# The first blocks of the triangular system made straight from PSUM, and the VectorE order of one head around them

## What is computed

```python
decay = jnp.exp(jnp.where(incl, gc[..., :, None] - gc[..., None, :], -jnp.inf))
k_beta = k * beta[..., None]
lower = jnp.where(strict, jnp.einsum('bnhid,bnhjd->bnhij', k_beta, k) * decay, 0.0)
sol = lax.linalg.triangular_solve(eye + lower, rhs, left_side=True, lower=True, unit_diagonal=True)
...
w_dec = sol[..., dv:]
k_dec = k * jnp.exp(gc[..., -1:] - gc)[..., None]
```

## Time and profile before

| | |
|---|---|
| median of 3 runs | 2103.08 us (2101.87 to 2104.11) |
| the profiled execution's own time | 2103.87 us |
| its span in the profile | 2102.2 us |
| TensorE matmul busy | 2072.2 us, 99% |
| TensorE weight load busy | 1687.8 us, 80% |
| VectorE busy | 1245.4 us, 59% |
| ScalarE busy | 804.9 us, 38% |
| GpSimd busy | 745.1 us, 35% |
| granted TensorE clock | 0.998 of full |
| share of the chain that ended last | PE 95%, VectorE 2%, DMA 1%, ScalarE 1% |

### The profile page before, as it was taken

The page is one execution under the profiler, slowest core; times in us unless marked ns, Lnnn a source line. Parts: engine busy times, 40 slices in busy tenths (PEclk is TensorE's granted clock), DMA queues, the critical chain, the costliest instruction groups (busy, mean ns, idle before and its releaser), DMA issues.

```text
span 2102.2 us, 30578 instructions
## 1 busy us (share of the span) xinstructions
PE 2072.2 (99%) x12076; PEld 1687.8 (80%) x12076; DVE 1245.4 (59%) x1739; ACT 804.9 (38%) x1055; POOL 745.1 (35%) x555
## 2 busy tenths in 40 slices
PE   6999999999999999999999999999999999999998
PEld 6789888887787787877878778777778888888886
DVE  6543243348779597795978959776433435454333
ACT  5433232344444443434434344453242222222223
POOL 0000000028577485774857748567201000100000
PEclk9999999999999999999999999999999999999999
DMA  8244343443433434334343343443356565553334
GB/s 257 62 125 131 105 130 90 115 118 97 118 101 96 119 96 116 101 99 120 95 114 102 104 115 100 110 116 101 105 165 205 171 188 151 175 152 110 114 123 148
DMA packets 382913, 260.63 MB, mean 124 GB/s; under 512 B 23769, under 2 KB 351810, under 8 KB 382146
## 3 DMA queue, kind: packets, MB, share of 16 engines
q1 hardware_dynamic: 364146, 203.16, 35.6%
q0 software_dynamic: 11408, 43.00, 6.0%
q10 hardware_dynamic: 7232, 12.72, 1.6%
HBM read 223.17 MB, written 27.28 MB: 119 GB/s over the span
## 4 chain that ended last, share of the span: by engine, by line
PE 95%; DVE 2%; DMA 1%; ACT 1%; issue 1%; POOLq 0%; ACTq 0%; DVEq 0%
PE bank L450 29%; PE bank L452 28%; PE bank L451 28%; PE bank L1089 1%; PE bank L848 1%; PE bank L863 1%; DMA yst<-s_out 1%; PE bank L971 1%; PE bank L983 1%; DVE wl L444 1%; PE bank L1038 0%; PE bank L1079 0%; PE bank L944 0%; PE bank L1052 0%; PE bank L1027 0%
## 5 line engine op out<-in xcount | busy, mean ns | idle before, releaser
L450 PE MATMUL bank<-uh,wh 128*128 128x512 f32 x2048 | 828.2, 404 | 3.3 <-DVE wl L444 2.9
L452 PE MATMUL bank<-uh,wl 128*128 128x512 f32 x2048 | 799.4, 390 | 0.0
L451 PE MATMUL bank<-ul,wh 128*128 128x512 f32 x2048 | 799.0, 390 | 0.0
L444 DVE TENSOR_TENSOR wl<-raw,wh 128x1024 fp32r<-128x1024 f32 x352 | 468.7, 1334 | 495.8 <-ACT wh L436 494.2
L436 ACT ACTIVATE wh<-raw 128x1024 fp32r<-128x1024 f32 x352 | 370.6, 1058 | 558.1 <-DMA raw<-in_w_in_dram 185.9
L450 PEld LDWEIGHTS bank<-uh,wh 128*128 128x128 f32 x2048 | 384.7, 188 | 92.3 <-issue 11.4
L452 PEld LDWEIGHTS bank<-uh,wl 128*128 128x128 f32 x2048 | 384.4, 188 | 83.3
L451 PEld LDWEIGHTS bank<-ul,wh 128*128 128x128 f32 x2048 | 385.2, 188 | 74.9 <-issue 2.9
L616 POOL DMA_DIRECT2D gated_c<-ox x8 | 4.3, 543 | 378.3 <-DVE ox L1780 377.8
L657 POOL TENSOR_TENSOR hr<-tcos,gr 128x512 f32<-128x512 f32 x32 | 51.7, 1617 | 199.4 <-DVE gi L2107 199.2
L1441 ACT ACTIVATE gk<-bank 128x512 f32<-128x512 f32 x48 | 28.7, 598 | 191.6 <-PE bank L452 191.5
(11 more groups left out here) (341 smaller groups left out, 2774.7 us busy)
## 6 DMA issues: line engine op xcount, KB each, us to landing
raw<-in_w_in_dram SPq DMA_DIRECT2D x224, 512.0 KB, 3.9
raw<-in_w_kv_mem_dram SPq DMA_DIRECT2D x32, 512.0 KB, 4.0
raw<-in_w_out_dram SPq DMA_DIRECT2D x32, 512.0 KB, 3.6
gates<-gk ACTq DMA_DIRECT2D x48, 256.0 KB, 4.3
gates<-gates POOLq DMA_DIRECT2D x24, 512.0 KB, 4.7
raw<-in_s_w_glu_dram SPq DMA_DIRECT2D x16, 512.0 KB, 4.0
raw<-in_w_br_c_dram SPq DMA_DIRECT2D x16, 512.0 KB, 4.0
raw<-in_w_br_a_dram SPq DMA_DIRECT2D x16, 512.0 KB, 3.9
```

What stands on the lines that cost most here:

```text
L444: dve.tensor_tensor(k.wl[slot][:, c], k.raw[slot][:, c], k.wh[slot][:, c].bitcast(F32), ALU.subtract).then_inc(k.w_lo, 1)
L450: pe.matmul(o, ah, bh, start=start, stop=False)
L451: pe.matmul(o, ah, bl, start=False, stop=False)
L452: return pe.matmul(o, al, bh, start=False, stop=stop)
```

## The change

It does three things.

1. `system` no longer makes all of `dl`. It makes the four 32-row diagonal strips of `lb` straight from bank 7 and `dl` (four multiplies of 32 x 128), and `first_blocks` loses its four copies. The full product into `dl` is a new function `masked_keys`. The order on VectorE becomes `system`, `first_blocks`, `masked_keys`, `keys`, `values`.
2. The copies `s5h`, `hph`, `dh` and `cwh` are gone; the instructions read the columns of `s5p`, `hp`, `prm2` and `prm1` at the head's index.
3. GpSimd's `arguments(0)` waits for the constant `s5_formed`, counted once before the mixer, in place of `sliced`. The count of `s5_w` is 12 for each head in place of 13.

```diff
 def system(j):
     dve.wait_ge(k.kk, count(j, 1, 1))
     dve.wait_ge(k.pm, count(j, 2, 4))
+    wait(dve, k.lx, count(j, 0, 6))
+    for r in range(0, P, B):
+        tt(k.lb[r:r + B, :, :], chunked(ps[7][:, :])[r:r + B, :, r:r + B], k.dl[r:r + B, :, r:r + B],
+           ALU.mult).then_inc(k.tu_s, 1)
+
+def masked_keys(j):
+    dve.wait_ge(k.tu_s, count(j, 4, 8))
     tt(k.dl[:, :, :], chunked(ps[7][:, :]), k.dl[:, :, :], ALU.mult).then_inc(k.lm, 1)

 def first_blocks(j):
-    dve.wait_ge(k.lm, count(j, 1, 1))
-    wait(dve, k.lx, count(j, 0, 6))
-    for r in range(0, P, B):
-        dve.tensor_copy(k.lb[r:r + B, :, :], k.dl[r:r + B, :, r:r + B]).then_inc(k.tu_s, 1)
     dve.wait_ge(k.tu_s, count(j, 4, 8))
     dve.transpose(k.lbt[:, :, :], k.lb[:, :, :]).then_inc(k.tu_s, 1)
...
-        if j: keys(j); system(j); values(j); first_blocks(j)
+        if j: system(j); first_blocks(j); masked_keys(j); keys(j); values(j)
...
-        if j: head_parameters(j)
...
-    wait(dve, k.ysum, count(j, 0, 1))
-    dve.tensor_copy(k.dh[:, :], k.prm2[:, 96:104][:, bass.ds(at(j), 1)]).then_inc(w, 1)
...
-        if heads: conv_weights(a); convolve(a, 0)
+        if heads: convolve(a, 0)
...
 # GpSimd, arguments(q)
-            hi_, lo_ = k.s5h[:, 1, q:q + 1], k.s5h[:, 2, q:q + 1]
+            hi_, lo_ = (k.s5p[:, n, 4 * at(j) + q:4 * at(j) + q + 1] for n in (1, 2))
...
-                wait_apart(k, pool, k.sliced, count(j, 2, 2))
+                pool.wait_ge(k.s5_formed, 2)
```

More of the change, by code:

```diff
@@ L205, in build @@
             k.zbs = sb(area, "zbs", [S])
-            k.cwh = sb(area, "cwh", [CONV, 3])
             k.braw = sb(area, "braw", [2, 4, GS])
@@ L230, in build @@
             k.st = sb(area, "st", [P])
-            k.hph = sb(area, "hph", [4, NT])
             k.hk = sb(area, "hk", [4, NT])
-            k.s5h = sb(area, "s5h", [5, 4])
-            k.dh = sb(area, "dh", [1])
             k.xb = sb(area, "xb", [S])
@@ L309, in build @@
             sems("mx_out", "zb_st", "pad_zero", "z_kept")
[L311 to L314, removed]
+        k.tu_zero, = \
+            sems("tu_zero")
+        k.s5_formed, k.conv, k.silu, k.sq, k.osum, k.grow_s = \
+            sems("s5_formed", "conv", "silu", "sq", "osum", "grow_s")
         k.grow_st, k.rsum, k.root, k.er_s, k.dd, k.dec, k.rn = \
@@ L537, in s5_loads @@
     def s5_loads(j):
-        wait_apart(k, sp, k.s5_w, count(j, 0, 13))
+        wait_apart(k, sp, k.s5_w, count(j, 0, 12))
         for n, b in enumerate((k.b_re, k.b_im)):
@@ L1061, in s5_matrices @@
     def s5_matrices(j):
-        pe.wait_ge(k.s5_w, count(j, 13, 13))
+        pe.wait_ge(k.s5_w, count(j, 12, 12))
         pe.wait_ge(k.bp_l, count(j, 2, 2))
@@ L1463, in input_halves @@
     def input_halves(j):
-        act.wait_ge(k.s5_w, count(j, 9, 13))
+        act.wait_ge(k.s5_w, count(j, 8, 12))
         wait(act, k.s5_tr, count(j, 0, 1))
@@ L1816, in s5_factors @@
             step(tt(T(11), T(11), T(12), op))
-            step(tt(k.s5p[:, 3 + n, :], T(11), T(9), ALU.mult))
+            tt(k.s5p[:, 3 + n, :], T(11), T(9), ALU.mult).then_inc(k.s5_formed, 1)
+            dve.wait_ge(k.s5_formed, n + 1)
     def delta_parameters():
@@ L1891, in rep_chunks @@
         return m.unsqueeze(1).to_broadcast([P, NT, n])
[L1893 to L1899, removed]
     def s5_matrices(j):
         w = k.s5_w
-        wait(dve, k.ysum, count(j, 0, 1))
-        dve.tensor_copy(k.dh[:, :], k.prm2[:, 96:104][:, bass.ds(at(j), 1)]).then_inc(w, 1)
         dve.wait_ge(k.s5_in, count(j, 64, 64))
-        cre, cim = (k.s5h[:, n, :].unsqueeze(2).to_broadcast([P, 4, GS]) for n in (3, 4))
+        cre, cim = (k.s5p[:, n, 4 * at(j):4 * at(j) + 4].unsqueeze(2).to_broadcast([P, 4, GS]) for n in (3, 4))
         br, bi = k.braw[:, 0, :, :], k.braw[:, 1, :, :]
@@ L1910, in s5_matrices @@
             tt(k.bt[:, n, :, :], b, c, ALU.mult).then_inc(w, 1)
-        dve.wait_ge(w, count(j, 5, 13))
+        dve.wait_ge(w, count(j, 4, 12))
         wait(dve, k.s5_tr, count(j, 0, 1))
@@ L1941, in convolve @@
         n = count(j, 4 * part, 12)
+        taps = k.prm1[:, 0:96].rearrange("p (n r h) -> p n r h", n=CONV, r=3)
         dve.wait_ge(k.mx_out, count(j, part + 1, PER))
@@ L1949, in convolve @@
             if t == 0:
-                ts(dst[:, :], src[:, 0:S], k.cwh[:, 0, part:part + 1], None, ALU.mult).then_inc(k.conv, 1)
+                ts(dst[:, :], src[:, 0:S], taps[:, 0, part, at(j):at(j) + 1], None, ALU.mult).then_inc(k.conv, 1)
                 continue
             dve.wait_ge(k.conv, n + t)
-            stt(dst[:, :], src[:, t:t + S], k.cwh[:, t, part:part + 1], dst[:, :], ALU.mult, ALU.add).then_inc(k.conv, 1)
+            stt(dst[:, :], src[:, t:t + S], taps[:, t, part, at(j):at(j) + 1], dst[:, :], ALU.mult, ALU.add).then_inc(k.conv, 1)
     def differences(j):
@@ L1959, in differences @@
         wait(dve, k.op, count(j, 0, 4))
-        tt(k.dl[:, :, :], k.gx[:, :, :], rows(k.hph[:, 1, :]), ALU.subtract).then_inc(k.dd, 1)
+        tt(k.dl[:, :, :], k.gx[:, :, :], rows(hp[:, 1, :, at(j)]), ALU.subtract).then_inc(k.dd, 1)
         dve.wait_ge(k.dd, count(j, 1, 3))
@@ L1978, in key_scales @@
         dve.wait_ge(k.rn, count(j, 6, 8))
-        tt(k.hk[:, 1, :], k.hk[:, 0, :], k.hph[:, 2, :], ALU.mult).then_inc(k.rn, 1)
-        tt(k.hk[:, 2, :], k.hk[:, 0, :], k.hph[:, 0, :], ALU.mult).then_inc(k.rn, 1)
+        tt(k.hk[:, 1, :], k.hk[:, 0, :], hp[:, 2, :, at(j)], ALU.mult).then_inc(k.rn, 1)
+        tt(k.hk[:, 2, :], k.hk[:, 0, :], hp[:, 0, :, at(j)], ALU.mult).then_inc(k.rn, 1)
     def values(j):
         dve.wait_ge(k.root, count(j, 1, 1))
-        tt(k.hk[:, 3, :], k.hk[:, 3, :], k.hph[:, 0, :], ALU.mult).then_inc(k.kscale, 1)
+        tt(k.hk[:, 3, :], k.hk[:, 3, :], hp[:, 0, :, at(j)], ALU.mult).then_inc(k.kscale, 1)
         dve.wait_ge(k.vtr, count(j, 1, 1))
@@ L2106, in s5_states @@
             for g in (gr, gi):
-                dve.tensor_tensor_scan(g[:, :], k.s5h[:, 0, q:q + 1].to_broadcast([P, S]), g[:, :], 0.0,
+                dve.tensor_tensor_scan(g[:, :], k.s5p[:, 0, 4 * at(j) + q:4 * at(j) + q + 1].to_broadcast([P, S]), g[:, :], 0.0,
                                        ALU.mult, ALU.add).then_inc(k.mod, 1)
```

5 lines of the change are left out of this document (1 added, 4 removed).

## The result

| | before | changed |
|---|---|---|
| median | 2103.08 us | 2126.51 us |
| lowest to highest, 5 runs each | 2101.87 to 2104.11 | 2123.33 to 2127.61 |
| ratio to before | | 1.0112, 95% interval 1.0100 to 1.0123 |
| span of the profiled execution | 2102.2 us | 2125.5 us |

The change makes the kernel 1.1% slower, by 23.4 us. 17.8 us were forecast (2120.9), and the time lies 0.5 us above the range (2107 to 2126). The direction and the place of the loss are as forecast; a cost that follows from it was left out, and the size is short by a quarter.

The account below looks back on a forecast made before the run. TensorE, busy 2072.2 of 2102.2 us, was taken to bound the kernel. Later `kd` cost 13.8 + 2.7 + 4.3 - 1.6 = 19.2, less 1.4 for the third state: +17.8 on 2103.1, 2120.9 us; range 2107 to 2126.

Parts of the forecast that it names:

- the slack of 2.1 us at L959: TensorE's matmul L959, second head: the product into `dl` ended at 620.76, L959 started at 622.88.
- the strips: VectorE's four 32 x 128 multiplies from PSUM in `system`: no overlap across partition quarters, 4 x 0.32, last ending at T + 1.24.
- Rival 1: The four strip multiplies overlap at 0.21 each, so one step passes ahead of GpSimd: +6.7 us, 2109.8; chance 0.17.
- the two level-0 steps: Inversion's first multiply and subtraction on VectorE: each waits for GpSimd's TENSOR_TENSOR, ending 0.15 behind it; 1.1 and 1.4 us.
- Rival 2: GpSimd does not hold the multiply and subtraction at level 0, 0.29 us each: +2.6 us, 2105.7; chance 0.14.
- the wait: TensorE waiting for `kd` before transposing `dl`: 2.3 us in six middle heads, 2.7 in the first, 4.3 more in the last.
- the small gains: Two TensorE delays expected to go: minus 1.6 us in the last head, minus 1.4 over seven heads.
- the half of `wl`: Last head, L444 at 1420.04: VectorE delivers some 3 us earlier relative to its block, so TensorE's wait goes, minus 1.6.
- the third state: TensorE's L1038: earlier `arguments(0)` no longer beside `bpad`, state over a microsecond earlier, 7 heads x 0.2 = minus 1.4.
- it is 2.25 late, and its weight load is no longer hidden, 0.06: TensorE's L959 in a middle head, starting at 625.13 instead of 622.88: 2.3 us per head, 13.8 for six.
- Rival 4: VectorE meets one more GpSimd instruction, as by `hk` with `vb` late for L952: 8 x 1.3 more, 2131; chance 0.06.
- The citation on the pipe: Skill rule that VectorE's next instruction starts only when the pipe is empty: 2.4 us more in sum; rejected from the rows.

Follow-up runs that it names:

- order taken back: Changed kernel with VectorE's keys ahead of everything and first_blocks behind values, strips still from PSUM: 2100.95 us, ratio 0.9993.
- the transpose behind: Changed kernel with the last transpose of level 0 of the inversion put behind keys on VectorE: 2122.89 us, ratio 1.0091.

## Why the prediction was wrong, point by point

**Right: what bounds the kernel, and where the loss is.** TensorE at 99%, a VectorE saving worth nothing, and the slack of 2.1 us at L959 used up by the eight instructions of the inversion and the product into `dl`, put ahead of `kd`. Measured: a wait in eight heads of eight, for `kd`; in seven it goes if either side is moved (order taken back, TensorE later).

**Right: the strips.** Four multiplies at 0.32, 1.24 us forecast, 1.23 measured, each from 270 to 296 ns. Rival 1, with 0.21, is refuted; the trace agrees with the rule on start quadrants.

**Right: the two level-0 steps.** Forecast: held until GpSimd's instruction ends, 0.15 behind it; measured 0.15 and 0.15. Rival 2 (they are not held) is refuted, and the run with GpSimd later shows what it would have given.

**Right in sign, a little small: the wait.** 2.3 forecast for a middle head, 2.44 measured. 0.11 of it is one distance: the product into `dl` starts 0.35 behind the transpose L2008, where I took the 0.24 of L2016 and L2017. The last head was forecast at 4.3 more than its earlier 1.5, that is 5.8, and has 5.92. Over all heads the waits came out 1.3 us above the forecast (22.1 for 20.8).

**Right: the small gains.** 1.6 for the half of `wl`, measured 1.7; 1.4 for the third state, measured 1.2. The cause of the second was wrong: the prediction gave it to the earlier `arguments(0)` and put the copies at zero, and the run with `arguments(0)` late keeps it (283 ns at the most, for 377). That the size came out is luck.

**Wrong: "it is 2.25 late, and its weight load is no longer hidden, 0.06".** The price of a wait was taken as its length and a weight load. The step that failed is that nothing was put behind the wait for TensorE itself: after waits of 2.93, 2.56 and 5.92 us its clock was at the lower level, and the projection behind it took 5.2 us more (with TensorE's busy time 4.4 up, where "unchanged" was forecast). The run with TensorE kept busy shows that the standing idle is the cause. The trace of before had no wait in the mixer over 1.6 us, and its clock there was 1.00 throughout. But it has one earlier, ahead of the mixer, at 16.12 us, with a window behind it:

```profile
16.12 0.36 PE L450 MATMUL bank<-mh,wh 128*128 128x256 f32 x1 [2.59 <-DVE wl L444]
```

```profile
16.40:19.80 3.40, 3.40 (x18) 3.40 (x17) 0.91 (x2) 0.91 (x2) 0.91 (x2) 0.51 1.34 297
```

That is half of the clock for 3.4 us, or 1.7 us as an estimate from this row, behind an idle time like the forecast one. It should have stood in the sum as a bound, 1.7 in each of up to eight heads. With the 5.2 us that were measured the forecast would have been 2126.1; the longer waits (+1.3) and the first round (-0.55) are most of the rest.

**The range.** It reached 0.6 us per head above the forecast and did not hold a cost outside the sum. Rival 4 (2131) was there as another mechanism and at 0.06.

**The citation on the pipe.** The Trainium skill, page VectorE: DVE Perf Modes, section The DRAIN you can't avoid, also says that an instruction that is not held starts earlier, which the prediction left out. With that its rule is what the rows show: 0.60 between starts of 0.68 us in both kernels.

## What to carry to other kernels

Before moving work ahead of a result, write down when each consumer asks for it on the engine that bounds the kernel: here 70 us of VectorE and GpSimd work were saved (1245.4 to 1193.0 us and 745.1 to 727.4), and 23 us lost, for an order in which the last result that one matmul needs came 4.4 us later against 2.1 us of slack. The cheapest cure was on the side that waits: TensorE asking two eighths later cost nothing that the times show and took away the whole loss, though a wait of 3.28 us stays in the last head. And a wait of the engine that bounds the kernel costs its length and, when it reaches a few us, possibly a slow stretch behind it: count both.

## What the runs showed of the hardware that I had not expected

TensorE's clock after a wait isn't decided by the length of that wait alone. In the run with the new system and order alone five waits of 2.43 to 2.45 us left it at 1.00 and one of 2.44, in the third head, did not; in the run with `values` ahead, six waits of 3.38 us each, behind the same work, gave 0.61, 1.00, 0.55, 0.64, 1.00 and 0.58; in the run with the transpose behind, 2.62 us left it alone and 2.09 us did not; 3.28 us left it alone in the last head of the run with TensorE asking later. After 3.9 us and more it fell each time. What else decides it was not found, and whether it makes such kernels scatter more isn't shown: the changed kernel's five runs lie within 4.3 us and the four with the transpose behind within 7.7, but 27 runs of the kernel before, beside the first experiments, lie within 5.1 (2101.22 to 2106.31).

A VectorE instruction that reads PSUM (the strips, 0.27 to 0.30 us; `kbg` and `kd`, 0.67 to 0.68) and VectorE's transposes (0.30 to 0.32) ran at their own pace beside GpSimd in every run, while a step with two inputs in SBUF was held to the end of the GpSimd TENSOR_TENSOR under way, even with 4 elements to do (L1984, 0.72 us).
